# Neighbourhood attention: queries and keys ahead of values, value projections inside the first four pairs of heads, bias in its own buffer

## The reference

```
h, hc     = modulated tokens and modulated context (256 x 1024 each)
rk rv nk nv (of h and hc), rq rg nq (of h)  = projections, 512 columns each
y_ret     = silu(rg) * head_norm(bidirectional retention(rq, rk, rv))       4 heads of 128
y_na      = softmax([nq nk^T/8 + bias, masked to a window | nq nkc^T/8]) @ [nv | nvc]    8 heads of 64
y         = [y_ret, y_na] @ w_out         (1024 x 1024)
x         = layer_norm(a * x + m * y);  then route tokens and run the experts
```

## Time and profile before

| | us |
|---|---|
| runs of the kernel before | 2233.53, 2235.29, 2239.97 (median 2235.29) |
| profiled execution, span from first to last instruction (the only time given for it) | 2236.3 |
| PE busy | 2093.8 (94%) |
| PEld busy | 1447.5 (65%) |
| DVE busy | 948.2 (42%) |
| ACT busy | 565.6 (25%) |
| POOL busy | 3.1 |
| mean DMA rate | 278 GB/s |

### The profile page before, as it was taken

One profiled execution on the slowest core, in us unless ns is written; L12 is line 12 of the kernel. 1 busy time (PEld: TensorE's weight loads), 2 busy tenths in 40 slices (PEclk: granted clock), 3 DMA queues, 4 the chain that ended last, 5 costly groups with the idle time before them and its releaser, 6 DMA issues.

```text
span 2236.3 us, 30643 instructions
## 1 busy us (share of the span) xinstructions
PE 2093.8 (94%) x12726; PEld 1447.5 (65%) x12726; DVE 948.2 (42%) x1872; ACT 565.6 (25%) x1056; POOL 3.1 (0%) x10
## 2 busy tenths in 40 slices
PE   7999999999999999999988899999987899999986
PEld 6867779998877789998976444433334544443333
DVE  7899735543643355566365422211113522111112
ACT  2124123331135033334344211111112311111112
POOL 0000000000000000000000000000000000000000
PEclk9999999999999999999999899999999999999999
DMA  6435654556435654432341899999999599999995
GB/s 269 152 151 226 257 232 151 188 188 261 153 113 238 253 205 174 176 140 96 113 180 63 362 422 427 426 428 427 426 426 387 198 424 425 427 426 428 425 426 220
DMA packets 50548, 621.05 MB, mean 278 GB/s; under 512 B 5616, under 2 KB 5616, under 8 KB 12560
## 3 DMA queue, kind: packets, MB, share of 16 engines
q1 hardware_dynamic: 49968, 615.79, 67.5%
q0 software_dynamic: 480, 3.87, 0.4%
HBM read 618.59 MB, written 1.05 MB: 277 GB/s over the span
## 4 chain that ended last, share of the span: by engine, by line
PE 69%; DMA 19%; DVE 9%; ACT 2%; issue 1%; SPq 0%; ACTq 0%; DVEq 0%
PE bank L636 19%; DMA ring<-in_experts 12%; PE bank L1294 11%; PE bank L1317 6%; DMA arena<-in_experts 6%; DVE wide L1958 3%; PE bank L849 3%; PE bank L850 3%; PE bank L851 3%; PE sums L851 3%; PE sums L850 3%; PE sums L849 3%; PE sums L1327 2%; PE bank L992 2%; PE bank L994 2%; PE bank L993 2%
## 5 line engine op out<-in xcount | busy, mean ns | idle before, releaser
L636 PE MATMUL bank<-h,ring 128*128 128x256 f32 x1568 | 347.1, 382 | 0.0
L636 PEld LDWEIGHTS bank<-h,ring 128*128 128x128 f32 x1568 | 298.1, 191 | 48.3 <-issue 6.5
L2195 DVE TENSOR_TENSOR ring_split<-ring,arena_split 128x2048 fp32r<-128x2048 f32 x64 | 144.1, 2289 | 150.1 <-ACT arena_split L1579 150.0
L2651 DVE TENSOR_TENSOR wide<-bank,wide 128x256 f32<-128x256 f32 x64 | 27.2, 425 | 394.1 <-ACT wide L1776 394.1
L2658 DVE SCALAR_TENSOR_TENSOR scratch_split<-bank,small,wide_split 128x512 fp32r<-128x512 f32 x64 | 48.1, 751 | 272.3 <-ACT wide_split L1784 272.3
L1579 ACT ACTIVATE arena_split<-ring 128x2048 fp32r<-128x2048 f32 x64 | 119.3, 1906 | 157.3 <-PE sums L851 144.0
L849 PE MATMUL bank<-h_split,arena_split 128*128 128x256 f32 x512 | 147.6, 288 | 7.1 <-DVE scratch_split L2218 7.1
L1294 PE MATMUL bank<-ring,h 128*64 128x512 f32 x640 | 143.6, 595 | 10.1 <-DMA ring<-in_experts 10.1
L850 PE MATMUL bank<-scratch_split,arena_split 128*128 128x256 f32 x512 | 146.7, 286 | 0.0
L851 PE MATMUL bank<-h_split,ring_split 128*128 128x256 f32 x512 | 146.5, 286 | 0.0
L849 PE MATMUL sums<-smax_split,arena_split 128*128 128x256 f32 x512 | 144.9, 283 | 0.0
(11 more groups left out here) (384 smaller groups left out, 3566.3 us busy)
## 6 DMA issues: line engine op xcount, KB each, us to landing
ring<-in_stream SPq DMA_DIRECT2D x99, 2048.0 KB, 7.8
ring<-in_experts SPq DMA_DIRECT2D x96, 2048.0 KB, 32.5
arena<-in_experts SPq DMA_DIRECT2D x72, 2048.0 KB, 31.0
arena<-in_experts SPq DMA_DIRECT2D x24, 1024.0 KB, 28.2
stat<-in_experts SPq DMA_DIRECT2D x24, 512.0 KB, 29.0
scratch<-in_experts SPq DMA_DIRECT2D x24, 512.0 KB, 30.8
arena<-in_stream SPq DMA_DIRECT2D x1, 2048.0 KB, 36.0
wide<-in_na_bias POOLq DMA_DIRECT2D x1, 1536.0 KB, 11.9
```

The costliest lines, as they stand in the source:

```text
L636: mm = pe.matmul(dst, a, b, start=(first and i == 0), stop=(i == len(terms) - 1))
L2195: dve.tensor_tensor(split["ring"][:, slot, 2048 * part:2048 * part + 2048], v, HI[("up", "down")[part]][:, j % 2, :].bitcast(F32), ALU.sub ...
```

## The change

On PE the queries are projected before the values, and the values' chunk comes last. The value projections are made block by block (`value_rows`): tokens 0 to 127 and 128 to 255 of the input, then the same of the context, one behind the scores of each of the pairs 0 to 3. ACT copies each of them out at the end of its work on that pair. The first output half moves from behind the scores of pair 1 to pairs 6 and 7, in two parts. The bias table has a buffer of its own (`extra`), is loaded early by SP, and all eight mask adds stand together on DVE ahead of the head norm. The output weights' high and low parts are made at other units. The transfers of POOL's queue move to SP's and ACT's queues. Some unchanged lines and moved definitions are cut from the diff:

```diff
-AB_CHUNK = {name: C_AB + c for c, name in enumerate(("rk", "rq", "rv", "rg", "nk", "nv", "nq"))}
+AB_CHUNK = {name: C_AB + c for c, name in enumerate(("rk", "rq", "rv", "rg", "nk", "nq", "nv"))}
...
-        shared = {"ring": [P, RING, CW], "h": [P, KT, T], "scratch": [P, KT, T], "arena": [P, 14464], "smax": [P, 6, 512],
-                  "wide": [P, 8192]}
+        shared = {"ring": [P, RING, CW], "h": [P, KT, T], "scratch": [P, KT, T], "arena": [P, 14336], "smax": [P, 6, 512],
+                  "wide": [P, 8192], "extra": [P, CW]}
...
-        W2["nbias"] = wide[:, 0:HEADS * 6 * GRID].rearrange("p (h e) -> p h e", h=HEADS)
+        W2["nbias"] = extra[:, 0:HEADS * 6 * GRID].rearrange("p (h e) -> p h e", h=HEADS)
@@ SP @@
                     load_chunk(n)
+                    if n == chunk_of(LAYERS - 1, "mod", MOD_MLP[0]):
+                        S.wait(sp, "mixed", LAYERS - 1)
+                        sp.dma_start(W2["ctx"], ctx_tokens).then_inc(S.sem("ctx_landed"), 16)
+                    if n == C_AB + 1:
+                        sp.dma_start(W2["nbias"], na_bias).then_inc(S.sem("na_bias_landed"), 16)
+                        S.wait(sp, "x_added", 1, "mlp")
+                        S.wait(sp, "mod_turned", 1)
+                        sp.dma_start(B["con2"], consts2).then_inc(S.sem("consts2_landed"), 16)
@@ POOL @@
-            pool.dma_start(pos_i[:, :], positions).then_inc(S.sem("positions_landed"), 16)
...
-            S.wait(pool, "mixed", LAYERS - 1)
-            pool.dma_start(W2["ctx"], ctx_tokens).then_inc(S.sem("ctx_landed"), 16)
-            S.wait(pool, "x_added", 1, "mlp")
-            S.wait(pool, "mod_turned", 1)
-            pool.dma_start(B["con2"], consts2).then_inc(S.sem("consts2_landed"), 16)
-            S.wait(pool, "filled", "nvc", 1)
-            pool.dma_start(W2["nbias"], na_bias).then_inc(S.sem("na_bias_landed"), 16)
@@ PE @@
             project("nk", 1)
             head_sums("sum", lambda hd: B["rkc"].rearrange("p a (b t) -> p (a b) t", b=2)[:, hd, :], ("retained",))
-            project("nv", 0)
+            project("nq", 0)
             head_sums("sum2", lambda hd: smax[:, hd // 2, T * (hd % 2):T * (hd % 2) + T], ("squares", "head"))
-            project("nv", 1)
-            project("nq", 0)
             project("nq", 1)
+
+            def value_rows(out_name, src, t):
+
+                n = AB_CHUNK["nv"]
+                bank = open_bank(pe, out_name, t)
+                for half in range(2):
+                    hi, lo = ab_weights(n, half, half)
+                    mm = row_half(bank, t, half, hi, lo, lambda k: V_HIGH[src][:, k, :], lambda k: V_LOW[src][:, k, :])
+                filled(mm, out_name, t)
+                if (out_name, t) == ("nvc", 1):
+                    for half in range(2):
+                        S.note(("ab_half", n, half), *S.at[("filled", "nvc", 1)])
+                    used_with(n, *S.at[("filled", "nvc", 1)])
+
+            value_fills = (("nv", "h", 0), ("nv", "h", 1), ("nvc", "ctx", 0), ("nvc", "ctx", 1))
...
-            def out_half(c, half, buf):
+            def out_half(c, half, buf, pairs=(0, 1)):
...
-                for i in range(2):
+                for i in pairs:
...
+                if 1 not in pairs:
+                    return
...
             for pair in range(8 + 3):
                 if pair < 8:
                     na_scores(pair)
-                if pair == 1:
+                if pair < 4:
+                    value_rows(*value_fills[pair])
+                if pair == 6:
                     pe.wait_ge(S.sem("ret_split"), S.value("ret_split", 0))
-                    out_half(0, 0, 0)
+                    out_half(0, 0, 0, (0,))
+                if pair == 7:
+                    out_half(0, 0, 0, (1,))
                 if 2 <= pair < 10:
                     na_turn(2 * pair - 4)
                     na_turn(2 * pair - 3)
+                if pair == 3:
+                    S.wait(pe, "projected", "nvc", 1)
                 if pair >= 3:
                     na_weigh(pair - 3)
@@ ACT @@
+            act.dma_start(pos_i[:, :], positions).then_inc(S.sem("positions_landed"), 16)
...
             next_high("nk", 1)
-            next_high("nv", 0)
             for i in range(2):
                 S.wait(act, "variance", "head", i)
                 S.give(act.activation(smax[:, 2 + i, :], smax[:, 2 + i, :], ACT.Sqrt), "root", "head", i)
-            keep("nv")
-            keep("nvc")
-            next_high("nv", 1)
             next_high("nq", 0)
             keep("nq")
+            next_high("nq", 1)
             act.wait_ge(S.sem("ret_ready"), S.value("ret_ready", 0))
             S.give(act.activation(flat2(Y_HIGH[:, 0:4, :]), flat2(B["rg"]), ACT.Copy), "ret_high", 0)
-            next_high("nq", 1)
+
+            def keep_values(name, t):
+
+                copy_out(B[name][:, t, :], lambda b: b[:, :], "projected", (name, t), (name, t))
...
-                if pair == 2:
+                if pair < 4:
+                    keep_values(("nv", "nvc")[pair // 2], pair % 2)
+                if pair in (3, 4):
+                    next_high("nv", pair - 3)
+                if pair == 8:
                     ab_high(C_ABOUT + 1, 0, 0, (C_ABOUT, 0))
@@ DVE @@
-            low("nv", 0)
-            low("nv", 1)
+            low("nq", 0)
+            low("nq", 1)
+
+            def mask_bias(hd):
+
+                v = W2["nbias"][:, hd, :].rearrange("p (e c) -> p e c", c=GRID)
+                link(dve.tensor_tensor(v, v, cst("na_mask").unsqueeze(1).to_broadcast([P, 6, GRID]), ALU.add))
+
+            dve.wait_ge(S.sem("na_bias_landed"), 16)
+            for hd in range(HEADS):
+                mask_bias(hd)
...
-            low("nq", 0)
...
             S.give(ins, "ret_ready", 0)
-            low("nq", 1)
+            low("nv", 0)
+            low("nv", 1)
...
-            ab_low(C_ABOUT, 0, 0)
...
-            dve.wait_ge(S.sem("na_bias_landed"), 16)
-            mask_bias(0)
...
-                if u < 1:
-                    mask_bias(1)
-                if u % 4 >= 2 and u < 14:
-                    mask_bias(2 * (u // 4) + u % 2 + 2)
-                if u == 3:
-                    ab_low(C_ABOUT, 1, 1)
-                if u == 5:
-                    ab_low(C_ABOUT + 1, 0, 0)
+                if u in (8, 10):
+                    ab_low(C_ABOUT, (u - 8) // 2, (u - 8) // 2)
...
             for pair in range(2, 4):
                 yn_low(pair)
+            ab_low(C_ABOUT + 1, 0, 0)
             ab_low(C_ABOUT + 1, 1, 0)
@@ host @@
-        nc = bacc.Bacc("TRN2", target_bir_lowering=False, num_devices=1)
+        nc = bacc.Bacc("TRN2", target_bir_lowering=False, num_devices=1, dynamic_dma_scratch_size=64)
```

More of the change, by code:

```diff
@@ L309, in two_blocks_kernel @@
         smax = whole["smax"]
+        extra = whole["extra"]
         stat = sb("stat", [P, 2, 512])
@@ L2391, in _ @@
                    "ret_split", 0)
-            ab_low(C_ABOUT, 0, 0)
-            def mask_bias(hd):
-                v = W2["nbias"][:, hd, :].rearrange("p (e c) -> p e c", c=GRID)
-                link(dve.tensor_tensor(v, v, cst("na_mask").unsqueeze(1).to_broadcast([P, 6, GRID]), ALU.add))
-            dve.wait_ge(S.sem("na_bias_landed"), 16)
-            mask_bias(0)
             def yn_low(pair):
```

## The result

The changed kernel takes **2257.05 us** (median of four runs, 2254.43 to 2258.56), the kernel before 2236.73 beside it: ratio 1.0087, 95% interval 1.0070 to 1.0105, so 20.3 us slower. I forecast 2250.7 with a range of 2240 to 2258. The sign and the range held; the forecast's own range (2246 to 2256) did not, and the time that rival C gave for long slow stretches (2255 to 2260) fits better than mine. The upper end of the range is 1 us away, and one of the four runs (2258.56) lies beyond it.

The account below looks back on a forecast made before the run. The mixer's end bounds the kernel, since expert transfers start there. Waits plus slow clock of 28.7 + 9.4 = 38.1 against 16.8 + 5.9 = 22.7 make it 15.4 us longer: 2251.7, or 2250.7 as median; range 2240 to 2258.

Parts of the forecast that it names:

- rival C: Slow stretches in the mixer are the long kind: 20 us or more slower, 2255 to 2260; chance 12%.
- What bounds the kernel: The mixer's end starts the transfer-filled expert stages; its gain or loss reaches the end one for one.
- Step 1: Before the second head sums: PE waits 3.0 + 0.5 us, as eight mask adds take DVE 4.6 us.
- Step 2: Before the first value block: PE waits 5.5 us, to 1137, for weight splits behind DVE's 9.5 us chain.
- step 6: Half clock after pauses: six stretches of 3.4 us at 1.6 each, 9.4 us; upper bound about 25.
- Step 3: Ahead of pair 3's scores and the first weighing: PE waits 3.9 us each for ACT's value block copies.
- Step 4: Rest of the attention loop: waits of 2.5 and 4.3 us at DVE's splits, the second shrinking by 1.6; tail 3.6.
- Step 5: Before the last output halves: PE waits some 3.0 us for a weight split behind the last low part.
- Its being on the path: Little of the 5.9 us of slow clock counts before; after, it falls on dense work PE itself delays.
- Moved transfers: Positions, context, bias and constants loaded through other queues: 0 us, with bounds of -0.5 and +0.5.
- Rival A: First value block: weights ready in time, blocks fill PE's waits; 8.3 us faster, about 2227; chance 8%.

Follow-up runs that it names:

- e1_mask: Changed kernel with the eight mask adds ahead of the second query weight split on DVE: 2249.76 us.
- e4_weights: Changed kernel with the values' weights split ahead of the head norm, whose reciprocal rounds move into the softmax loop: 2251.38 us.
- e2_keep: Changed kernel with ACT's copies of the third and fourth value block ahead of its turns and exps in pairs 2 and 3: 2248.07 us.
- e9_before_warm: Kernel before with unused matmuls in its three attention pauses, overfilled (18.3 us of fill in 10.6 of pauses): 2239.31 us.
- e5b_sized: Changed kernel with unused matmuls, sized to fit, in five of PE's long pauses to keep the clock up: 2251.08 us.
- e9b_sized: Kernel before with unused matmuls, sized to fit, in its three longest attention pauses: 2235.06 us.
- e6_transfers: Kernel before with only the bias in its own buffer and POOL's transfers moved to SP and ACT: 2237.93 us, ratio 1.0004.
- e8_all: Changed kernel with mask adds, value copies, last output split and value weights all made earlier, two output splits behind units 7 and 12: 2229.70 us, ratio 0.9973.

## Why the prediction was right, and what was mis-sized

- **What bounds the kernel: held.** Every stage that shrank took the time with it, to within 3 us, and the fillers' gain did too. The experts began at 1239.64, or 1241.6 with the 2.0 us by which this trace ran early (I said near 1235).
- **Step 1, the adds:** predicted waits 3.0 + 0.5; measured 3.4. e1_mask shows that the place of the adds makes them.
- **Step 2, the values' weights:** predicted 5.5, measured 5.3. e4_weights takes all but 0.8 away. The end of the wait agrees with my 1137 only by luck: 1136.6 is 1138.6 with the 2.0 us, 1.6 late. Most of that are the 1.25 us that DVE waited for head sums at half clock, which step 6 took for hidden behind DVE's chain; they lengthened the chain. The wait stayed 5.3 because PE, too, came late.
- **Step 3, the value blocks:** predicted 3.9 and 3.9, both for ACT's copy; measured 3.9 and 3.8, for the instruction named. e2_keep takes both away. In full they cost 9.0 us in the medians, more than the 7.8 of waiting.
- **Step 4:** predicted 2.5 and 2.7, tail 3.6; measured 2.0, 2.7 and 3.3. Held.
- **Step 5:** predicted 3.0, measured 3.1. Held.
- **Step 6, the clock: the mis-sized term.** I priced six stretches of 3.4 us at 1.6 us each, 9.4 in all. Seven came, four of them 6.8 us long. Full-clock busy time of the stage is 91.6 - 5.9 = 85.7 by the prediction's own account (85.3 in e9_before_warm), so after has 102.3 - 85.7 = 16.5 us of slow clock. Waits and slow clock are then 27.7 + 16.5 = 44.2 against 22.7 before: +21.5, where I had +15.4. As written, the waits were 1.0 too high and the slow clock 7.1 too low. Counted alike it is less: the prediction leaves a seventh stretch, of 1.6, inside its waits, so that it has 27.1 of waits and 11.0 of slow clock, 0.6 and 5.5 too low. I took the shorter kind though the one long stretch of the earlier trace rows stood behind the longest pause; four of after's pauses (5.3, 3.9, 3.8 and 2.7 us) were followed by a long one. The upper bound in step 6 (25) was for just this, and rival C with its 12% should have had more. How many stretches are long is in part chance (see Open), so that the 20.3 us lie inside my range by some luck too.
- **Its being on the path: right.** e5b_sized keeps 8.6 of 11.4 us, e9b_sized at most 1.1 of 3.4. I put the difference down to what follows a pause: value blocks and outputs that PE alone delays in after, pairs that DVE delays in before. That is argued; no run moves one kind of work behind the other's pause.
- **Moved transfers: 0,** within the interval of e6_transfers (-1 to +3 us), which is wider than my bounds of 0.5.
- **Rival A (the interleaving pays):** wrong for the change as made, right in its mechanism. I named one place as deciding, the first value block. e4_weights alone repaired it and the kernel was still 0.7% slower. With all four places repaired, and two output splits moved, it is 6 to 8 us faster than before, where rival A's sum gave 8.3; whether three with the first value block among them would do was not run. The Trainium skill's advice that interleaving regimes may improve performance ("Perfetto Trace Analysis", Optimization Strategy) came true in e8_all and not in the change as made (20.3 us slower). What the same section goes on to ask, to find what each gap waits for and make it start sooner, is what the repairs do.
- **Open:** why a slow stretch is 3.4 or 6.8 us long behind like pauses (behind the last outputs' pause of 3.1 us it was 3.4 in after and e4_weights, 6.8 in e1_mask, e2_keep and e5b_sized); what moving the first output half to pairs 6 and 7 does by itself, which no run tests; and why the part behind the stage varies by 5 us between executions. e5b_sized saved 8.6 in its stage and 6.0 in the medians; the intervals are too wide to say more.

## What to carry to other kernels

Work interleaved into another engine's loop needs everything that feeds and drains it moved with it: list for each moved block which engine prepares its weights and which copies its result, and what stands ahead of those two instructions in their engines' order. Here eight adds, three weight splits and two copies in the wrong place made a change 20 us slower that is 6 to 8 us faster with them and the head norm's last steps moved. Price a new pause of TensorE at more than its length when work that only TensorE delays follows it: here 10.9 us of added waiting brought 10.6 us of slow clock with it.

## What the runs showed of the hardware

- The f32 matmul of 128x128 by 256 columns that the fillers use shows as two instructions, 0.43 us together at full clock from start to start, 0.46 with the end of the chain shared out (14 instructions took 3.19 us).
- A pause of 2.0 us in after (up to 1186.20) was followed by a granted clock of 0.55, as was one of 1.8 in the earlier trace rows. Pauses of 1.7 in the earlier trace rows, of 1.9 in e9_before_warm (up to 1151.13) and of 2.0 in e5b_sized (up to 1187.04) were not, nor were those of 0.8 and 0.9 us in e8_all. All pauses of 2.7 us and more in the stages of after and of its repairs were.
- With the same PE instructions up to the mixer, single executions reached it up to 4.9 us apart.
